# A two-layer loop written out on all engines, with four transposes moved into the last chunk of a layer

## The reference

```python
def hybrid_layer(x, ...):
    h = rms_norm(x, attn_norm)
    qa, ka, va, qd, kd, vd = split(h @ w_in)          # w_in 1024 x 3072, 16 heads of 64
    qa, ka, qd, kd = rope(...)                        # on heads
    out_a = rms_norm(moba_attention(qa, ka, va), moba_out_norm)       # 8 heads, causal
    out_d = rms_norm(dilated_attention(qd, kd, vd), dil_out_norm)     # 8 heads, dilated
    x = x + concatenate([out_a, out_d]) @ w_out       # 1024 x 1024
    h = rms_norm(x, mlp_norm)
    x = x + square(relu(h @ w_up)) @ w_down           # 1024 x 4096, 4096 x 1024
    return x

for l in range(2):
    x = hybrid_layer(x, ...)
return rms_norm(x, final_norm)
```

## Time and profile before

| what | value |
|---|---|
| time, median of 3 runs | 629.52 us (628.9 to 630.27) |
| time of the profiled execution | 630.27 us |
| its span, from the first to the last instruction | 628.4 us |
| PE busy | 611.8 us, 97% |
| DVE, ACT, POOL busy | 384.7, 317.0, 49.4 us |

### The profile page before, as it was taken

The page is one execution under the profiler, slowest core; times in us unless marked ns, Lnnn a source line. Parts: engine busy times, 40 slices in busy tenths (PEclk is TensorE's granted clock), DMA queues, the critical chain, the costliest instruction groups (busy, mean ns, idle before and its releaser), DMA issues.

```text
span 628.4 us, 9521 instructions
## 1 busy us (share of the span) xinstructions
PE 611.8 (97%) x3161; PEld 507.0 (81%) x3161; DVE 384.7 (61%) x604; ACT 317.0 (50%) x532; POOL 49.4 (8%) x46
## 2 busy tenths in 40 slices
PE   7999999999999999999989999999999999999995
PEld 6877787888888888888867787788888888888883
DVE  2774565588765565656377546756876575655634
ACT  3746466656463543534166455674753543535422
POOL 1330122001000000000004201300100000000001
PEclk9999999999999999999999999999999999999998
DMA  8843344227755646465237335242496646465201
GB/s 299 319 152 130 134 134 135 76 88 274 250 183 187 213 145 231 158 215 186 70 108 268 115 118 198 70 133 68 142 319 192 217 144 236 155 194 206 100 0 68
DMA packets 58659, 104.18 MB, mean 166 GB/s; under 512 B 1744, under 2 KB 34816, under 8 KB 58624
## 3 DMA queue, kind: packets, MB, share of 16 engines
q1 hardware_dynamic: 57712, 102.31, 48.4%
q10 hardware_dynamic: 912, 1.43, 0.6%
HBM read 102.69 MB, written 1.05 MB: 165 GB/s over the span
## 4 chain that ended last, share of the span: by engine, by line
PE 88%; issue 4%; POOL 3%; DVE 2%; ACT 2%; POOLq 0%; ACTq 0%; DVEq 0%
PE psum L877 19%; PE psum L752 17%; PE psum L754 17%; PE psum L753 17%; PE psum L879 10%; PE psum L822 2%; PE psum L759 1%; POOL roped L328 1%; PE psum L839 1%; PE psum L838 1%; PE psum L813 1%; PE psum L858 1%; PE psum L854 1%; PE psum L837 1%; POOL rope_r L339 1%
## 5 line engine op out<-in xcount | busy, mean ns | idle before, releaser
L512 DVE TENSOR_TENSOR w_lo<-raw,w_hi 128x1024 fp32r<-128x1024 f32 (+1 forms) x192 | 231.9, 1244 | 54.3 <-ACT w_hi L377 54.3
L377 ACT CAST w_hi<-raw 128x1024 fp32r<-128x1024 f32 x192 | 191.1, 1050 | 10.8 <-DMA raw<-in_w_in 8.2
L877 PE MATMUL psum<-xt,w_hi 128*128 128x512 f32 x512 | 179.6, 394 | 0.0
L879 PE MATMUL psum<-xt,w_lo 128*128 128x256 f32 x512 | 142.7, 279 | 0.0
L877 PEld LDWEIGHTS psum<-xt,w_hi 128*128 128x128 f32 x512 | 95.9, 187 | 22.0
L754 PE MATMUL psum<-w_hi,h_lo 128*128 128x512 f32 x256 | 101.1, 395 | 0.0
L753 PE MATMUL psum<-w_lo,h_hi 128*128 128x512 f32 x256 | 101.1, 395 | 0.0
L752 PE MATMUL psum<-w_hi,h_hi 128*128 128x512 f32 x256 | 101.0, 394 | 0.0
L879 PEld LDWEIGHTS psum<-xt,w_lo 128*128 128x128 f32 x512 | 96.5, 188 | 1.4
L752 PE MATMUL psum<-w_hi,xt 128*128 128x512 f32 x192 | 80.9, 421 | 4.5 <-DVE xt L518 2.8
L457 ACT COPY up_cross<-psum 128x512 f32<-128x512 f32 x32 | 18.8, 587 | 121.2 <-PE psum L879 121.2
(11 more groups left out here) (85 smaller groups left out, 602.6 us busy)
## 6 DMA issues: line engine op xcount, KB each, us to landing
raw<-in_w_up SPq DMA_DIRECT2D x32, 1024.0 KB, 5.6
raw<-in_w_down SPq DMA_DIRECT2D x32, 1024.0 KB, 6.7
raw<-in_w_in SPq DMA_DIRECT2D x22, 1024.0 KB, 5.5
raw<-in_w_out SPq DMA_DIRECT2D x8, 1024.0 KB, 4.9
raw<-in_w_in SPq DMA_DIRECT2D x4, 512.0 KB, 5.8
x<-in_x SPq DMA_DIRECT2D x1, 512.0 KB, 4.8
x<-in_x ACTq DMA_DIRECT2D x1, 512.0 KB, 8.3
final_gain<-in_final_norm SPq DMA_DIRECT2D x1, 512.0 KB, 5.6
```

The source lines that it names most:

```text
L377: act.copy(w_hi[:, slot, part], raw[:, slot, part]).then_inc(hi_done, 1)
L512: dve.tensor_tensor(w_lo[:, slot, part], raw[:, slot, part], w_hi[:, slot, part].bitcast(F32), ALU.subtract).then_inc(split_done, 1)
L877: pe.matmul(out, w_hi[:, slot, cols], xt[:, k, :, :].rearrange("p a b -> p (a b)"), start=k == 0, stop=False)
L879: last = pe.matmul(out[:, SEQ:2 * SEQ], w_lo[:, slot, cols], xt[:, k, 0, :], start=False, stop=k == KT - 1)
```

## The change

The loop over the layers becomes a loop of the program that writes the kernel: all five engines get two copies of the layer's instructions, with constants where registers were. The MLP loop inside each layer stays a loop of the device. In the same edit the first four block transposes of the next layer's x (8 transpose instructions on PE), the four remainders on DVE that go with them and the first half unit's `lo` are moved to the end of the layer before. On PE the transposes now stand ahead of the last output block (1, 1) of the last `down`, behind a wait for `x_updated`. On DVE, `lo` stands ahead of the four adds and the remainders ahead of the last add. ACT's order stays as it was.

```diff
-            with sp.Fori(0, DEPTH) as l:
+            for l in range(DEPTH):
...
-            with pool.Fori(0, DEPTH) as l:
+            for l in range(DEPTH):
...
-            with act.Fori(0, DEPTH) as l:
+            for l in range(DEPTH):
...
-            with dve.Fori(0, DEPTH) as l:
-                dve.wait_ge(gains_done, l + 1)
-                x_to_lo(l, TR_X, x_banks, 0, 0)
-                lo(l, 0, 0, 0, BANK)
-                for k in range(1, 4):
-                    x_to_lo(l, TR_X, x_banks, k, 0)
+            for l in range(DEPTH):
+                if l == 0:
+                    dve.wait_ge(gains_done, 1)
+                    x_to_lo(l, TR_X, x_banks, 0, 0)
+                    lo(l, 0, 0, 0, BANK)
+                    for k in range(1, 4):
+                        x_to_lo(l, TR_X, x_banks, k, 0)
                 lo(l, 0, 0, 1)
...
                 h_to_lo(l, UPS - 1, 1)
+                if l + 1 < DEPTH:
+                    lo(l + 1, 0, 0, 0, BANK)
                 dve.wait_ge(rstd_done, l * STATS + ST_M + 1)
                 for n in range(2):
                     for t in range(TOK):
                         if (n, t) == (1, 1):
+                            if l + 1 < DEPTH:
+                                for k in range(4):
+                                    x_to_lo(l + 1, TR_X, x_banks, k, 0)
                             dve.wait_ge(weights_used, used(l, UNITS - 1))
...
                     for n in range(2):
                         for t in range(TOK):
+                            if (n, t) == (1, 1) and l + 1 < DEPTH:
+                                pe.wait_ge(x_updated, l * 4 + 6)
+                                turn_x(x_banks, range(4))
                             for j in range(2):
...
-            with pe.Fori(0, DEPTH) as l:
+            for l in range(DEPTH):
                 for s in range(4 * IN_CHUNKS):
-                    if s in (0, 2):
-
-                        wait_all(pe, (x_loaded[s // 2], 16), (x_updated, l * 4 + s + 2))
-                        if s == 2:
-
-                            pe.wait_ge(turned_lo, l * TRS + TR_X + 4)
-                        turn_x(x_banks, range(2 * s, 2 * s + 4))
+                    if s == 0 and l == 0:
+                        pe.wait_ge(x_loaded[0], 16)
+                        turn_x(x_banks, range(4))
+                    if s == 2:
+                        pe.wait_ge(x_loaded[1], 16)
+                        pe.wait_ge(x_updated, l * 4 + 4)
+                        pe.wait_ge(turned_lo, l * TRS + TR_X + 4)
+                        turn_x(x_banks, range(4, KT))
                     project_in(l, s)
```

## The result

The changed kernel takes 624.22 us (median of 6, 623.62 to 624.73), the kernel before beside it 629.56 (6 runs, 628.9 to 631.09). The ratio is 0.9907, with an interval of 0.9897 to 0.9918; on 629.52 that is 623.7 us, 0.3 under the low end of my range. The profiled execution took 623.63 us.

What follows compares the result with a forecast made beforehand. PE, busy 611.8 of 628.4 us, was taken to bound the kernel, so only its pauses could be won. Terms of 3.0 + 0.5 = 3.5 us off 629.52 gave 626.0 us, range 624.0 to 627.9 for 8 in 10.

Steps and rivals of the forecast that it cites:

- The start and the end: SP's loop set-up ahead of the first weight load and the loop exit after layer 1: counted nothing, 0.4 us at most.
- my likeliest case: The forecast's main case for the whole kernel: 624.9 to 626.8 us, a gain of 2.7 to 4.6 us; 74%.
- The loop's end and the moved transposes: Where the layers meet, PE's pause for DVE's remainder and the idle time before the transposes go: 3.0 us, 2.88 to 3.12.
- Registers inside the layers: Register instructions between links of the RoPE and `probs` chains fall away, shortening PE's waits: 0.5 us, bounds 0 and 2.5.
- The attention waits: Rival: PE's waits for `roped` and `probs` go altogether, 3.0 + 2.5 = 5.5 us, giving 624.0 us; 10%.
- part of the pause: Rival: ACT or DVE reaches moved work late, so some of PE's pause between layers returns; 628.0 with 1.5 us; 8%.
- The idle "issue": Rival: DVE's idle 2.44 us between layers is not the branch but moves along; the 2.82 us pause stays, 629.5; 4%.
- The MLP loops: Rival: inner loops at new addresses pay 2.08 to 2.44 us per uncovered jump back, up to 24 us, 650; 4%.

Runs made afterwards that it cites:

- the two edits: Only SP's layer loop written out in the kernel before: 628.55 us, ratio 0.9976; SP's layer loop put back in the changed kernel: 624.96 us, 0.9919.
- the last version: The changed kernel with ACT's sums of squares of x in layer 0 moved ahead of the rounding of chunk 1: 623.21 us, ratio 0.9893.

## Why the prediction missed

**The step that failed** is "The start and the end": "I count nothing, 0.4 at most". The start gave 1.90 us in the means of the profiles; 1.48 of it is ACT's first rounding (at 8.75 in the mean of the four profiles before, 7.27 of the two after). Without the 1.90 the profiles' sum of 5.86 would be 3.96, inside the 2.7 to 4.6 of my likeliest case. I took SP's 0.3 us of loop set-up as a delay that the 6.8 us between issue and use would swallow. The runs showed the reverse: issued 0.3 us earlier, the data were in use 1.1 us earlier in the means of the seven profiles of each kind, and the first RoPE transposes follow that first rounding by 22.7 to 23.5 us in ten of the thirteen profiles ahead of the last version (by 24.5 and 24.6 in two, where PE's slower pace lasted longest, and by 22.1 in one). What this loop on SP is worth in time is 0.7 to 1.5 us by the two edits. What brought the rest of the 1.90 is open, and so is which transfers the first load goes ahead of; taking the masks away from them changed nothing.

**The second miss has no term in my sum**: the clock behind the pause. My rows had a granted clock of 1.00 there, from an execution without a fall. In the means it adds 0.77 us (1.49 and 1.59 over 121.78, in two of four).

**The loop's end and the moved transposes: right.** 3.0 us with bounds of 2.88 to 3.12; measured 3.09, of which DVE's jump is 2.3 and the move 0.75. The hand-overs came as worked out: the first remainder is ready at 311.61 + 0.48 = 312.09 and asked for at 312.96, 0.87 in hand (0.8 to 1.0 forecast); the moved `lo` on DVE is done at 305.45, the first add starts at 308.17.

By the 0.11 us that the Trainium skill gives a compare-and-branch ("Advanced Engine Details and Errata", section "Control Flow Timing") DVE's loop would, by estimate, have been worth a tenth of a microsecond; the run has 2.3, so the measurement decides. The Trainium skill, "Runtime: NRT & Kernel Launch", section "Instruction fetch mechanics", says that a jump to code outside the window waits for a fetch. The trace agrees as far as the jump's 2.3 us and fewer instruction packets go; the queue of the earlier trace rows now reads

```profile
q14 instruction: 11, 0.09, 0.0%
```

with 11 packets for 17. With DVE's loop alone written out it has

```profile
q14 instruction: 14, 0.11, 0.1%
```

and with SP's alone 17. The moment fits too, which the prediction had left open: in all five profiles with DVE's jump where the layers meet, one packet of this queue falls into DVE's idle time there (before: between 316.3 and 318.7 us); with DVE's loop alone written out none is moved between its last add and PE's first projection (313.9 to 316.3).

**Registers inside the layers: half or less of 0.5.** Layer 1's attention has 121.65 and 121.62 us against 121.81 and 121.75 in profiles without a fall of the clock: 0.14. In layer 0 it is 0.08. This term was too large, so the two misses above are larger together than the total shows. RoPE's wait in layer 1 went from 0.4 to 0.17:

```profile
331.88 0.66 PE L819 MATMUL psum<-ident,roped 128*128 128x128 f32 x4 [0.17 <-POOL roped L328]
```

and that of layer 0 is set by the start, 1.30 in one profile, 0.17 in the other.

**The rivals.** The attention waits did not go altogether: `probs` still costs 1.6 us, and the `row_bias` of 0.88 us before it still takes 0.81. That rival's 624.0 lies nearest to the result, for a reason that didn't happen: that is luck. No part of the pause came back. The idle "issue" was the jump, as DVE alone shows. The MLP loops did not slow: 168.07 and 168.08 against 167.93 to 168.02 in layer 0, at most 0.15 us.

## What to carry to other kernels

Where an engine stands idle on "issue" at a loop's end and another waits for it, price the jump from that row, and add what the waiting TensorE may lose behind the pause: one profile can show a clock of 1.00 there and the next one half of it. Before counting a few tenths at the start of a queue at nothing, take several profiles and follow the first load to its first user; what left the queue 0.3 us earlier was here used 1.1 us earlier in the mean. And a median that moves by more than the pause removed is a reason to profile the kernel before again.

## What the runs showed of the hardware

- A jump back over a long body cost DVE 2.3 us between two instructions (2.44 with it, 0.12 without; 2.37 to 2.65 in the five profiles with it).
- After PE had stood still for 2.8 to 3.1 us, the granted clock was at 0.50 for a stretch in three of six profiles, and layer 1's attention took 1.2 to 1.6 us longer. In one of them PE had first done four products at the upper level (318.62 to 319.65). The Trainium skill, "TensorE: Matmul & The Clock Gate", section "Wait — 56ns, not 53.3ns?", has 427 and 216 ns from start to start for 512 columns at the two levels; the traces agree with 0.42 to 0.43 and have 0.23 us.
- The pace of the first products varied for one and the same kernel. From 12 to 16 us two profiles of the kernel before read:

```profile
12.00:16.00 4.00, 4.00 (x13) 3.04 (x12) 2.67 (x5) 1.35 (x2) 0.00 (x0) 0.57 1.05 394
```

```profile
12.00:16.00 4.00, 4.00 (x23) 3.38 (x22) 2.36 (x4) 1.83 (x4) 0.00 (x0) 1.00 1.05 394
```

The first is the third profile, the second the one before it; 13 instructions of PE against 23 in the same 4 us. In the third PE had stood still for 3.56 us ahead of these products, in the second for 1.03.
